# Convolution taps summed in PSUM with eight products added on GpSimd, one projection unit split instead of native, and another unit's low half built by DMA

## The reference

```
h = rms_norm(x); proj = h @ w_in                      # 1024 x 5120
a, bv, bg, z = split(proj, [1024, 1024, 1024, 2048])
pooled = trailing mean over 2, 4, 8, 16 tokens - token    # one window per group of 256 channels
ya = (pooled @ pool_w per group) * pool_scale
u  = bv * sigmoid(bg)
u  = causal depthwise conv, 31 taps (u) + bias
yb = silu(layer_norm(u))
x  = x + (concat(ya, yb) * silu(z)) @ w_out           # 2048 x 1024
```

## Time and profile before

| | |
|---|---|
| median of 3 runs | 331.78 us (331.74 to 331.89) |
| the profiled execution | 331.88 us, of which the span of its instructions is 330.1 us |
| PE busy | 323.8 us (98%), 2212 matmuls |
| DVE busy | 256.1 us (78%) |
| ACT busy | 230.4 us (70%) |
| POOL busy | 51.3 us (16%), nearly all in issuing DMAs |
| mean granted clock of PE | 0.997 of full |

### The profile page before, as it was taken

One profiled execution on the slowest core, in us unless ns is written; L12 is line 12 of the kernel. 1 busy time (PEld: TensorE's weight loads), 2 busy tenths in 40 slices (PEclk: granted clock), 3 DMA queues, 4 the chain that ended last, 5 costly groups with the idle time before them and its releaser, 6 DMA issues.

```text
span 330.1 us, 5760 instructions
## 1 busy us (share of the span) xinstructions
PE 323.8 (98%) x2212; PEld 295.0 (89%) x2212; DVE 256.1 (78%) x475; ACT 230.4 (70%) x429; POOL 51.3 (16%) x58
## 2 busy tenths in 40 slices
PE   7999999999999999999999999999999999999995
PEld 7899999999989999998989999988887777778885
DVE  2799989999689999996886899647556787748633
ACT  4687999994999897945785457824746667576630
POOL 0050024324422310120000000005400140500000
PEclk9999999999999999999999999999999999999998
DMA  7989488979999997676639344790634323300003
GB/s 275 412 283 347 151 275 212 203 172 343 278 250 341 175 387 289 130 174 209 255 115 382 140 134 132 265 363 2 254 127 148 129 111 131 122 0 2 2 0 127
DMA packets 12842, 64.77 MB, mean 196 GB/s; under 512 B 1424, under 2 KB 1552, under 8 KB 6544
## 3 DMA queue, kind: packets, MB, share of 16 engines
q1 hardware_dynamic: 8064, 53.78, 43.7%
q0 software_dynamic: 4608, 10.49, 17.4%
q10 hardware_dynamic: 144, 0.15, 0.2%
HBM read 52.88 MB, written 1.05 MB: 163 GB/s over the span
## 4 chain that ended last, share of the span: by engine, by line
PE 87%; DMA 4%; DVE 3%; ACT 3%; issue 1%; ACTq 0%
PE bank L1060 24%; PE bank L1061 23%; PE bank L1062 23%; PE bank L1094 4%; DMA w_lo<-raw 3%; PE bank L1120 2%; PE bank L1168 2%; PE bank L1274 2%; PE bank L1301 2%; PE bank L1137 2%; PE bank L1287 2%; DMA X<-xT 1%; PE bank L1253 1%; ACT scratch L467 1%; DVE scratch L754 1%
## 5 line engine op out<-in xcount | busy, mean ns | idle before, releaser
L725 DVE TENSOR_TENSOR w_lo<-raw,w_hi 128x1024 fp32r<-128x1024 f32 x76 | 90.2, 1219 | 19.1 <-ACT w_hi L459 18.8
L1060 PE MATMUL bank<-h_hi,w_hi 128*128 128x256 f32 x304 | 86.7, 285 | 0.3 <-DMA w_lo<-raw 0.3
L459 ACT CAST w_hi<-raw 128x1024 fp32r<-128x1024 f32 x84 | 84.3, 1047 | 2.7 <-PE bank L1062 2.7
L1062 PE MATMUL bank<-h_hi,w_lo 128*128 128x256 f32 x304 | 86.0, 283 | 0.0
L1061 PE MATMUL bank<-h_lo,w_hi 128*128 128x256 f32 x304 | 86.0, 283 | 0.0
L1060 PEld LDWEIGHTS bank<-h_hi,w_hi 128*128 128x128 f32 x304 | 58.3, 192 | 0.7 <-issue 0.7
L1061 PEld LDWEIGHTS bank<-h_lo,w_hi 128*128 128x128 f32 x304 | 58.3, 192 | 0.1
L1062 PEld LDWEIGHTS bank<-h_hi,w_lo 128*128 128x128 f32 x304 | 58.3, 192 | 0.0
L843 DVE SCALAR_TENSOR_TENSOR scratch<-scratch,params 128x256 f32<-128x256 f32 x108 | 44.0, 477 | 0.2
L1060 PE MATMUL bank<-w_hi,h_hi 128*128 128x512 f32 x96 | 39.2, 408 | 0.0
L1060 PE MATMUL bank<-ya_hi,w_hi 128*128 128x256 f32 x128 | 38.1, 297 | 0.0
(11 more groups left out here) (106 smaller groups left out, 544.6 us busy)
## 6 DMA issues: line engine op xcount, KB each, us to landing
raw<-w SPq DMA_DIRECT2D x49, 1024.0 KB, 6.4
side_v<-side_ring POOLq DMA_DIRECT2D x24, 256.0 KB, 8.2
w_lo<-raw POOLq DMA_DIRECT2D x8, 512.0 KB, 7.9
X<-xT SPq DMA_DIRECT2D x2, 512.0 KB, 5.2
out<-X SPq DMA_DIRECT2D x4, 256.0 KB, 2.7
consts<-const SPq DMA_DIRECT2D x1, 290.0 KB, 13.6
params<-vec ACTq DMA_DIRECT2D x1, 149.0 KB, 4.9
```

The lines of the kernel that those rows point to most:

```text
L459: nc.scalar.copy(halves(w_hi, cut_slot(n), half), halves(raw, n % RAW, half)).then_inc(hi_cut, 1)
L725: nc.vector.tensor_tensor(halves(w_lo, cut_slot(n), half), halves(raw, n % RAW, half), halves(w_hi, cut_slot(n), half).bitcast(F32), ALU.s ...
L1060: nc.tensor.matmul(dst, wh, ah, start=start, stop=False, skip_group_check=True)
L1062: return nc.tensor.matmul(dst, wl, ah, start=False, stop=stop, skip_group_check=True)
```

## The change

- Unit 9 leaves `NATIVE` and is split. Unit 12 becomes an `ADDED` unit; units 10 and 14 are cut in the plain way. ACT cuts unit 12 in slot 9, ahead of the copy of unit 9's result.
- Up to slot 18 the cut weights use four places of `w_hi` and `w_lo` in place of three.
- The first tap and DVE's taps of pair p are summed in PSUM bank 4+p (`partial`) up to slot 13; in slot 14 four DVE instructions add each bank to the sums in `V` ("merges"). PE waits for them before unit 16, which writes those banks.
- Eight tap products, which ACT makes with the four taps that start `V`, are added by GpSimd in `V`, two at a time in slots 4, 6, 8 and 13. They wait for DVE's cuts of that slot (`pool_gate`).
- POOL's side DMAs of slot n are issued one slot's code later, and from slot 4 on some stand behind the adds.
- `MEAN_AT` moves from (2, 0, 1) to (2, 0, 5) and `SUM2_AT` from (2, 1, 6) to (3, 0, 2).

```diff
-NATIVE = frozenset((0, 9, 13, 16, 21, 23, 25))
-EARLY_ADDED = (10, 14)
+NATIVE = frozenset((0, 13, 16, 21, 23, 25))
+EARLY_ADDED = (12,)
 ADDED = EARLY_ADDED + (22, 24)
+FOUR, SLOT_ORDER = ZA[1], (3, 2, 0, 1)
...
+POOL_ADDS = {4: (0, 0), 6: (0, 1), 8: (1, 2), 13: (2, 3)}
+POOL_STARTS = {3: (0,), 5: (1,), 7: (2,), 11: (3,)}
...
+        for pair in range(4) if n == MERGE_SLOT else ():
+            tiles = CONV_PAIRS[pair]
+            count += 1
+            plan[n].append((tiles, None, None, max(last[c] for c in tiles), count))
...
-MEAN_AT = 2, 0, 1
-SUM2_AT = 2, 1, 6
+MEAN_AT = 2, 0, 5
+SUM2_AT = 3, 0, 2
...
+        def partial(tiles):
+
+            c = tiles[0]
+            at = S * (c % 2)
+            t = bank[4 + c // 2][:, at:at + S * len(tiles)]
...
+            def pool_conv(n):
+
+                gate = pool_gate(n)
+                if gate and POOL_PLAN[n - 1]:
+                    pool.wait_ge(pooled if gate[0] == "pooled" else lo_cut, gate[1])
+                for pair, k, made, ready, _ in POOL_PLAN[n - 1]:
...
+                    pool.wait_ge(pool_product, made)
+                    nc.gpsimd.tensor_tensor(V[:, 2 * pair:2 * pair + 2, :], V[:, 2 * pair:2 * pair + 2, :],
+                                            pool_home(made), ALU.add).then_inc(pool_tap, 1)
...
+                for pair, k in POOL_START.get(n, ()):
+                    act.wait_ge(u_ready, pair + 1)
+                    for c in CONV_PAIRS[pair]:
+                        nc.scalar.mul(V[:, c, :], U[:, c, k:k + S], column(CW + TAPS * c + k)).then_inc(pool_started, 1)
...
-                if m in A:
+                if m in A and n + 2 not in EARLY_ADDED:
                     window_sums(m - A[0])
...
+                    if k is None and product is None:
+                        dve.wait_ge(pool_tap, POOL_LAST[c // 2])
+                        nc.vector.tensor_tensor(V[:, c:c + 2, :], total, V[:, c:c + 2, :], ALU.add).then_inc(tap, 1)
...
+                pe.wait_ge(tap, MERGED[g])
```

More of the change, by code:

```diff
@@ L113, in slot_free @@
     if n == SPARE:
-        return released(PW)
+        return released(max(m for m in CUTS if m <= FOUR and cut_slot(m) == CUT - 1))
     if n == Z1[3]:
@@ L149, with pool_products, pool_gate @@
 SIDE_ITEMS = 14
-PRODUCTS = 4
-LATE_RING = 4
+RINGS = (0, (1, 2, 3)), (A[0], (2, 3)), (A[1], (3, 4)), (ZB[0], (4,)), (ZB[1], (4, 5, 6, 7))
 LATE_SLOT = A[3] + 3
+MERGE_SLOT = PW - 2
+POOL_ADDS = {4: (0, 0), 6: (0, 1), 8: (1, 2), 13: (2, 3)}
+POOL_STARTS = {3: (0,), 5: (1,), 7: (2,), 11: (3,)}
+def pool_products():
+    plan, starts, taken, count, made, last = {}, {}, {pair: 0 for pair in range(4)}, 0, 0, {}
+    for n in range(BG[1], MERGE_SLOT + 1):
+        for pair in POOL_STARTS.get(n, ()):
+            starts[n] = starts.get(n, ()) + ((pair, FIRST_POOL[pair]),)
+            taken[pair], last[pair] = taken[pair] + 1, 0
+        plan[n - 1] = []
+        for pair in POOL_ADDS.get(n, ()):
+            made, count = made + 1, count + 1
+            plan[n - 1].append((pair, FIRST_POOL[pair] - taken[pair], made, last[pair], count))
+            taken[pair], last[pair] = taken[pair] + 1, count
+    return plan, starts, taken, last
 def side_taps(pair):
     return range(TAPS - SIDE_ITEMS, TAPS) if pair < SIDE else ()
+FIRST_POOL = [TAPS - 1 - (SIDE_ITEMS if pair < SIDE else 0) for pair in range(4)]
+POOL_PLAN, POOL_START, POOL_TAKEN, POOL_LAST = pool_products()
+POOL_USED = [done for items in POOL_PLAN.values() for _, _, _, _, done in items]
+def pool_gate(n):
+    if n - 1 in A:
+        return "pooled", n - A[0]
+    return ("cut", 2 * low_cuts(n + 2) + 2) if n + 2 not in NATIVE and n + 2 not in ADDED else None
 def side_items(n):
     return [(pair, n - BG[pair + 1]) for pair in range(SIDE) if 0 <= n - BG[pair + 1] < SIDE_ITEMS]
[L165 to L169, removed]
 def slot_work(n):
@@ L192, in conv_plan @@
 def conv_plan():
-    plan, last, used, count, before, late, folded = {}, {}, [], 0, None, None, []
-    left = {pair: [k for k in range(1, TAPS) if k not in side_taps(pair)] for pair in range(4)}
+    plan, last, used, count, before, late, folded, homes, free_at = {}, {}, [], 0, None, None, [], [], []
+    left = {pair: list(range(1, FIRST_POOL[pair] - POOL_TAKEN[pair] + 1)) for pair in range(4)}
     folds = [2 * pair + (SIDE_ITEMS + i) % 2 for pair in range(SIDE) for i in range(2)]
@@ L203, in conv_plan @@
         act_time = min(act_time, ACT_CARRY) + ACT_SHARE * length - act
+        for pair in range(4) if n == MERGE_SLOT else ():
+            tiles = CONV_PAIRS[pair]
+            count += 1
+            plan[n].append((tiles, None, None, max(last[c] for c in tiles), count))
+            dve_time -= 0.61
+            last.update({c: count for c in tiles})
+        if n == MERGE_SLOT:
+            merged = range(count - 3, count + 1)
         while dve_time > 0 or n == OA[0]:
@@ L216, in conv_plan @@
                 used.append(count)
+                ring = next(homes for first, homes in reversed(RINGS) if n >= first)
+                homes.append(ring[len(homes) % len(ring)])
+                free_at.append(max([u for u, h in zip(used[:-1], homes[:-1]) if h == homes[-1]], default=0))
                 dve_time, act_time = dve_time - 0.61, act_time - 0.8
@@ L829, in taps @@
             def taps(n):
-                for tiles, k, product, ready, _ in CONV_PLAN.get(n, ()):
+                for tiles, k, product, ready, done in CONV_PLAN.get(n, ()):
                     c = tiles[0]
```

78 lines of the change are left out of this document (52 added, 26 removed).

## The result

| | before | after |
|---|---|---|
| median of 9 runs | 331.78 us (331.49 to 332.09) | 333.86 us (332.45 to 334.65) |
| profiled execution, its span | 331.88, 330.1 us | 332.45, 330.5 us |
| matmuls of PE | 2212 | 2228 |

The ratio is 1.0057, 95% interval 1.0039 to 1.0074: slower, by more than the 0.2% that count here as no change. The forecast was 332.1 us with a range from 331.6 to 334.0. The result lies 0.14 us inside the upper end, but "same" was the likeliest case (0.57) and did not come; "slower" had 0.35.

The account below looks back on a forecast made before the run. PE, busy 323.8 of 330.1 us, was taken as the bound, with a rigid 20.24 us chain from mean to unit 26. -1.15 - 0.29 + 1.73 = +0.29 us gave 332.1 us, range 331.6 to 334.0.

Parts of the forecast that it names:

- -1.15 - 0.29 + 1.73 = +0.29 us: Whole sum: unit 9 split saves 1.15, unit 14's DMA wait goes (0.29), the mean four native matmuls later costs 1.73.
- The mean's term: Mean matmul four native matmuls later on PE, 0.432 us each: +1.73 us relative to the start of unit 23.
- The two gains together: Unit 9 split in place of native, 1.15 us, and unit 14's DMA wait gone, 0.29 us; 1.44 us.
- The rigid chain: From the mean at 149.47 to unit 26 at 169.71, 20.24 us across engines, unedited; PE's other work only accompanies it.
- The rival that PE keeps what it saves: Chain behind the mean isn't rigid, so PE keeps its 1.44 us: 330.3 us; chance 0.08.
- DVE's taps in PSUM, "I take 0": DVE taps summed in a PSUM bank cost nothing extra; fold for the mean near 148, 1.6 us to spare.
- a pass of cancelling counts: DVE's plan from unit 15's cut on: two pairs more and four singles fewer cancel, so the fold stays near 148.
- GpSimd's adds, "I take 1.4": GpSimd's eight adds into V take 1.4 us each, at no cost on the path unless they delay POOL's queued DMAs.
- The rival's mechanism: GpSimd's adds hold up DVE's cuts or window sums: about 2 x 2 us less 1.6 to spare, 334.5; chance 0.08.
- Unit 12's low half by DMA ... I take 0: Transfer on POOL's queue lands likely at 77.8, PE needs it at 80.15; cost 0, upper end 1.1 us.
- The rival for this: Unit 12's low half lands late and PE stalls before the mean: likely 333, up to 334.1; chance 0.15.
- the margin of 2.3 us: Time between unit 12's low half landing, likely at 77.8, and PE's need for it at 80.15.

Follow-up runs that it names:

- e3: The kernel before with only MEAN_AT and SUM2_AT moved to the change's new places; 333.53 us, ratio 1.0049.
- e4: The changed kernel with the four side DMAs of slots 8 and 9 issued behind unit 12's two DMAs; 332.42 us, ratio 1.0013.
- e5: e4 with the mean at slot 2, group 3 and the sum of squares at slot 2, group 7; 333.20 us, ratio 1.0036.
- e8: The changed kernel without the wait that keeps GpSimd's adds behind DVE's cuts; 336.57 us, ratio 1.0152.
- e1: The changed kernel timed again with no edit; 333.30 us, ratio 1.0054.
- e2: The changed kernel with the mean and the sum of squares back in their old places; 333.01 us, ratio 1.0035.
- e6: The changed kernel with GpSimd's eight adds on 4 of 256 columns a tile; 332.61 us, ratio 1.0031.
- e10: e4 with PE's 12 warm-up matmuls of 128 columns cut into 28 of 54; 340.81 us, ratio 1.0268.
- e12: e5 with 2 warm-up matmuls of 128 columns in place of 12; 333.44 us, ratio 1.0053.
- e7: The kernel before with eight more GpSimd adds at 22 to 37 us in a buffer not otherwise used then; 336.33 us, ratio 1.0141.
- e11: e5 with PE's 12 warm-up matmuls of 128 columns cut into 28 of 54; 339.83 us, ratio 1.0243.
- e9: The kernel before with PE's 12 warm-up matmuls of 128 columns cut into 20 of 76; 337.19 us, ratio 1.0156.

## Why the prediction was right or wrong

**"-1.15 - 0.29 + 1.73 = +0.29 us"**: right to within 0.1 us once the two other effects are taken away. The mean's term alone is e3's +1.72. The two gains together are e3's mean span less e4's, 331.68 - 330.27 = 1.41 us, against 1.44. All three are e4's mean span, +0.22 us. That the result as a whole lies in the range is partly luck: the sum was +0.29 us and the median moved by +2.08, and of what the sum lacked only one part was among the rivals.

**The rigid chain, "the distance from the mean to unit 26 is 20.2 us"**: 20.24 measured. The rival that PE keeps what it saves is out. PE's waits in the chain sum to 1.9 us, 2.07 predicted; the mean stood at 149.99, predicted 149.8, and later by just the 0.2 us that PE waited at 80.

**DVE's taps in PSUM, "I take 0"**: right. The taps cost 3 ns more each, 33 of them 0.1 us. By the Trainium skill's page "VectorE: DVE Perf Modes", section on the TRN2 errata, it would have been an estimated 65 ns each; no row here shows that, neither for writing with reading of a bank nor for reading alone, and the measurement decides. The fold came at 149.07, not near 148: a pass of cancelling counts didn't cover a wait of 1.57 us for an ACT product before 129.57 us. It ate most of the slack, which is why e5 gained so little.

**GpSimd's adds, "I take 1.4"**: 1.29 us. They cost nothing on the path, but only because the change fences them off from DVE's cuts. The rival's mechanism is real, and e8 prices it at about 3 us, more than the 2.4 us it was given.

**"Unit 12's low half by DMA ... I take 0"**: the range held, but this is the step of the sum that failed. I took the landing as the median of the eight in the trace of before (7.9 us), and looked at whether the DMAs ahead had been *issued*. They were in flight. The landings were 10.0 to 11.8 us in the traces with that order (after, e1, e2, e6, e8), and with the side DMAs behind 5.2 to 6.1 us in e4 and e5 and up to 7.4 in e10 to e12. The wait of PE near 80 us is the very sign that the prediction had named for this rival. PE's wait was 0.2, 0.5, 1.6, 0.3 and 0.8 us in these traces, and by mean spans it was worth 331.33 - 330.27 = 1.1 us for after and 331.12 - 330.27 = 0.8 us for e1, which ran beside e4 (some of it may be the end's, as e5's). The rival for this had 0.15 and "likely 333", of which the size was right; its chance should have been far above that, since the margin of 2.3 us was less than half of the landings' own spread.

**What no step had**: 0.3 to 0.7 us in the mean (e4 and e1), up to 1.6 in a run, at the end of the program. The 16 added matmul records of unit 9's split brought PE's program to the length at which this appears; that it is the time of a last block of instructions is the likely reading. I counted instructions by their duration only.

In sum, by means: +0.2 by the steps, +1.1 for unit 12 and +0.5 for the end make +1.8, against +1.88 (333.67 - 331.79). The first two are parts of the same difference of spans, so only the split between them, by e4, is a finding.

No kernel that beats the one before was found. The pieces suggest one: e5's work ends at a span of 329.8 us when the end is quiet, which with 1.82 us outside makes an estimated 331.6 us, 0.05% under 331.78 and less than this measurement can tell.

## What to carry to other kernels

A DMA that depends on a queue is priced by what is still in flight on that queue, not by what stands in it unissued: put the transfer that the bottleneck waits for ahead of the ones that nobody waits for yet. A saving ahead of a rigid chain between engines is worth only what the chain's start gains, so look first for which engine holds that start (here DVE's fold) and then place the matmul. Where runs scatter and the trace doesn't, compare time and span run by run, and look for instruction fetches near the end.

## What the hardware showed that was not expected

- Time outside the span is 1.74 to 1.84 us in the kernel before (44 runs), e3, e7 and e12, 1.79 to 1.93 us in e10 and e11, and 1.76 to 3.42 us in the programs of 2228 matmul records of PE. At times the extra lies inside the span (e5: 4.7 us for 3.1).
- Transfers on POOL's queue: 10.0 to 11.8 us behind four others of 256 KB, 5.2 to 7.4 without them, for the same 512 KB.
- An add on GpSimd and DVE's two-input work in SBUF lengthen each other, 1.29 to 1.82 us and 0.41 to 0.93 us (eight taps in 3.25 and 7.43 us), while DVE's work with an operand in PSUM is untouched (0.68 us in e7, six taps in 2.45 us in e8). Sums in PSUM are thus a way to run both side by side.
- Narrower float32 matmuls of PE with a new weight load each are no shorter: the warm-up takes 4.59 us for 24 records of 128 columns (after), 8.81 us for 40 of 76 (e9) and 12.20 us for 56 of 54 (e10), 0.19, 0.22 and 0.22 us each.
